# Mixer A probabilities of the sample tiles: from TensorE transposes to a round trip through DRAM and a 32x32 block transpose on VectorE

## The reference, cut to what matters

```
z = h @ w_in                       # q, k, v, gates of both mixers; h = modulated RMS norm of x
# mixer A, 8 heads, each with two 64-wide halves c of q and k; v is 128 wide
s = einsum('bqhcd,bshcd->bhcqs', q, k) / sqrt(64)
p = softmax(s, axis=-1)
p = p[:, :, 0] - lam[h] * p[:, :, 1]
o = einsum('bhqs,bshe->bqhe', p, v)      # sample: 512 + 256 keys; prompt: 128 keys
o = rms_norm(o, subln) * (1 - lam_init) * silu(gate)
y = rms_norm(x + gate_ada * (concat(o_A, o_B) @ w_out), g_final)
```

## Time and profile before

| | |
|---|---|
| median of 3 runs | 1253.91 us (1253.86 to 1254.21) |
| span of the profiled execution, first to last instruction | 1253.5 us |
| its own time outside the span | not shown; the median lies 0.4 us above the span |
| TensorE busy | 1222.7 us, 98% |
| VectorE, ScalarE, POOL busy | 800.0 (64%), 619.1 (49%), 258.3 us (21%) |
| chain of work that ended last | 92% TensorE |
| transposes of p on TensorE | 400 of 128x128, 192 of them for mixer A's sample tiles |

### The profile page before, as it was taken

The page is one execution under the profiler, slowest core; times in us unless marked ns, Lnnn a source line. Parts: engine busy times, 40 slices in busy tenths (PEclk is TensorE's granted clock), DMA queues, the critical chain, the costliest instruction groups (busy, mean ns, idle before and its releaser), DMA issues.

```text
span 1253.5 us, 16906 instructions
## 1 busy us (share of the span) xinstructions
PE 1222.7 (98%) x6251; PEld 991.3 (79%) x6251; DVE 800.0 (64%) x1242; ACT 619.1 (49%) x1296; POOL 258.3 (21%) x439
## 2 busy tenths in 40 slices
PE   5899999999999999999999999999999999999996
PEld 3455778888888888888888888888888888888885
DVE  4455488667586776755546374554647675789774
ACT  5522325645555465565556555656556765312223
POOL 1211033012031040222221221222223322211111
PEclk9999999999999999999999999999999999999998
DMA  9999242222221232322222121222224423756544
GB/s 348 371 377 349 84 110 76 62 71 74 76 96 44 67 106 53 100 60 83 71 61 86 51 91 51 82 59 83 59 72 133 139 83 98 254 187 228 184 135 177
DMA packets 130482, 156.45 MB, mean 125 GB/s; under 512 B 8304, under 2 KB 97040, under 8 KB 129632
## 3 DMA queue, kind: packets, MB, share of 16 engines
q1 hardware_dynamic: 116528, 109.60, 26.7%
q0 software_dynamic: 13424, 45.20, 11.4%
q10 hardware_dynamic: 448, 0.57, 0.1%
HBM read 144.18 MB, written 11.16 MB: 124 GB/s over the span
## 4 chain that ended last, share of the span: by engine, by line
PE 92%; SPq 3%; DVE 2%; DMA 1%; ACT 1%; POOL 1%; issue 0%; POOLq 0%; DVEq 0%; ACTq 0%
PE z_ps L704 24%; PE z_ps L706 23%; PE z_ps L705 23%; PE ring L795 5%; PE ring L884 4%; SPq L658 2%; PE ring L829 2%; PE ring L828 2%; PE ring L730 2%; PE ring L888 2%; DMA ada_raw<-in_w_ada_dram 1%; PE ring L706 1%; PE ring L705 1%; PE ring L891 1%; PE ring L704 1%
## 5 line engine op out<-in xcount | busy, mean ns | idle before, releaser
L704 PE MATMUL z_ps<-w_hi,xt_hi 128*128 128x512 f32 x1350 | 554.1, 410 | 2.6 <-issue 1.1
L706 PE MATMUL z_ps<-w_hi,xt_lo 128*128 128x512 f32 x1350 | 527.7, 391 | 0.0
L705 PE MATMUL z_ps<-w_lo,xt_hi 128*128 128x512 f32 x1350 | 527.2, 391 | 0.0
L1007 ACT ACTIVATE w_hi<-w_raw 128x512 fp32r<-128x512 f32 x270 | 169.3, 628 | 334.9 <-PE z_ps L706 309.2
L704 PEld LDWEIGHTS z_ps<-w_hi,xt_hi 128*128 128x128 f32 x1350 | 254.0, 188 | 68.1 <-issue 27.2
L1441 DVE TENSOR_TENSOR w_lo<-w_raw,w_hi 128x512 fp32r<-128x512 f32 x270 | 196.8, 732 | 162.6 <-ACT w_hi L1007 162.2
L706 PEld LDWEIGHTS z_ps<-w_hi,xt_lo 128*128 128x128 f32 x1350 | 253.4, 188 | 55.3
L705 PEld LDWEIGHTS z_ps<-w_lo,xt_hi 128*128 128x128 f32 x1350 | 254.8, 189 | 38.8
L1542 DVE TENSOR_REDUCE small<-s_sb 128x2 f32<-128x1536 f32 (+1 forms) x60 | 87.6, 1460 | 20.6 <-ACT s_sb L1007 20.6
L1153 ACT ACTIVATE s_sb<-s_sb,small 128x768 f32<-128x768 f32 (+1 forms) x120 | 98.0, 821 | 3.6 <-DVE small L1542 3.5
L1902 POOL TENSOR_TENSOR sg<-sg,zs 128x128 f32<-128x128 f32 (+1 forms) x60 | 38.6, 644 | 276.2 <-DVE sg L1511 275.6
(11 more groups left out here) (196 smaller groups left out, 1378.3 us busy)
## 6 DMA issues: line engine op xcount, KB each, us to landing
w_raw<-in_w_in_dram SPq DMA_DIRECT2D x188, 256.0 KB, 3.1
ada_raw<-in_w_ada_dram SPq DMA_DIRECT2D x64, 512.0 KB, 11.6
w_raw<-in_w_out_dram SPq DMA_DIRECT2D x64, 256.0 KB, 3.8
gate_raw<-in_w_ada_dram POOLq DMA_DIRECT2D x12, 1024.0 KB, 8.0
w_raw<-in_w_in_dram POOLq DMA_DIRECT2D x20, 256.0 KB, 6.3
o_spill<-row_st POOLq DMA_DIRECT2D x14, 320.0 KB, 3.4
row_st<-o_spill POOLq DMA_DIRECT2D x14, 320.0 KB, 3.3
x_sb<-in_x_sample_dram SPq DMA_DIRECT2D x4, 1024.0 KB, 9.6
```

What stands on the lines that cost most here:

```text
L704: pe.matmul(out, hi_l, hi_r, start=start, stop=False)
L705: pe.matmul(out, hi_l, lo_r, start=False, stop=False)
L706: return pe.matmul(out, lo_l, hi_r, start=False, stop=stop)
L1007: return act.activation(out, in_, ACT.Copy, **kw)
```

## The change

For the sample tiles of mixer A (t > 0, 32 tiles) the piece T has no TensorE work any more. ScalarE writes the scores in another order of columns (by quadrant i, key block k, 32 columns b). When the combine is done, SP stores the 128x768 tile to DRAM (`p_spill`), waits until it has landed, and loads it back in four DMAs, one for each group of 32 partitions, so that the 32x32 blocks stand in their places. One `transpose` on VectorE (`turn_blocks`) then turns every block and writes `pt_f`. It stands in the step where T stood, after `gated`. V(t) waits for it by `p_turned`. ScalarE's two copies from PSUM are gone; the third score copy becomes two. SP's program interleaves these transfers with its weight loads. In the last pass S(0) comes in step 3 instead of 4, S in 3, 4, 6, 8, 9 and V in 6, 8, 10, 12, 13. Tile 0 and mixer B stay as they were.

```diff
+LAST_STEPS = {
+    1: [("O", -1)], 2: [("QK", 0)], 3: [("S", 0)], 4: [("S", 1)], 5: [("T", 0)], 6: [("S", 2), ("V", 0)], 7: [("T", 1)],
+    8: [("S", 3), ("V", 1)], 9: [("T", 2), ("S", 4)], 10: [("V", 2)], 11: [("T", 3)], 12: [("V", 3), ("T", 4)], 13: [("V", 4)],
+    14: [("O", 0)], 15: [],
+}
+LAST_PLACES = {12: [2], 13: [4], 14: [2, 3]}
...
     if kind == "T":
-        return (2 if t else 1) * (2 if g == "G" and t else 1)
+        return 0 if by_blocks(a, t) else (2 if t else 1) * (2 if g == "G" and t else 1)
...
+            def move_blocks(a, t):
+
+                b, n = t % 2, p_count(a, t)
+                sp.wait_ge(p_ready, n_step(a, t) + 1)
+                sp.dma_start(p_spill[b], s_sb[:, b, 0, :]).then_inc(p_out[b], 16)
+                if n > 1:
+                    sp.wait_ge(p_turned, turns_before(a, t) - 1)
+                else:
+                    wait_full(sp, TURN[("V", D_IT - 1, TILES - 1)])
+                sp.wait_ge(p_out[b], 16 * n)
+                for i in range(QUAD):
+                    src = p_spill[b].rearrange("(j b) (i n) -> i b j n", j=QUAD, i=QUAD)[i]
+                    sp.dma_start(p_blocks[b][SUB * i:SUB * (i + 1), :, :], src).then_inc(p_in[b], 16)
...
+            for q in range(OPEN, len(ORDER)):
+                moves = [(a, t) for kind, a, t in steps_at(*ORDER[q - 1]) if kind == "S" and by_blocks(a, t)]
+                if moves:
+                    while j <= min(q // 2 + 3, len(ORDER) // 2 - 1):
+                        load_w(sp, j)
+                        j += 1
+                for a, t in moves:
+                    move_blocks(a, t)
...
                     wait_free(pe, m)
+                if by_blocks(a, t):
+                    pe.wait_ge(p_turned, turns_before(a, t) + 1)
...
+                if by_blocks(a, t):
+                    if t > 2:
+                        act.wait_ge(p_out[t % 2], 16 * p_count(a, t - 2))
...
+            def turn_blocks(a, t):
+
+                b = t % 2
+                dve.wait_ge(p_in[b], 16 * QUAD * p_count(a, t))
+                wait_full(dve, TURN[("V", a, t - 1)])
+                dve.transpose(pt_f[:, :].rearrange("p (k j b) -> p j k b", k=KB, j=QUAD),
+                              p_blocks[b][:, :, :].rearrange("p j (k b) -> p j k b", k=KB)).then_inc(p_turned, 1)
...
                     for kind, a, t in old:
                         if kind == "V":
                             gated(a, t)
+                for kind, a, t in late:
+                    if kind == "T" and by_blocks(a, t):
+                        turn_blocks(a, t)
```

More of the change, by code:

```diff
@@ L111, with by_blocks @@
 STEPS_D[2] = [("QK", 0)]
[L113 to L121, removed]
+LAST_STEPS = {
[4 more added lines that the diff above has]
+LAST_PLACES = {12: [2], 13: [4], 14: [2, 3]}
+QUAD, KB, SUB = 4, LAT + PAST, P // 4
+def by_blocks(a, t):
+    return t > 0 and group_kind(a) == "D"
 def group_kind(a):
@@ L303, in build @@
     gate_rows = nc.dram_tensor("gate_rows", (2, D_MODEL), F32).ap()
+    p_spill = nc.dram_tensor("p_spill", (2, P, NKEY), F32).ap()
     at = [(nc.sbuf_base + 31) // 32 * 32]
@@ L349, in build @@
     pt_f, _ = place("pt_f", [P, NKEY], F32, pt0)
+    p_blocks = [place(f"p_blocks{i}", [P, QUAD, KB * SUB], F32, pt0 + 4 * NKEY * (1 + i))[0] for i in range(2)]
     v_f, _ = place("v_f", [P, 7, DH], F32, pt0 - 4 * 7 * 2 * DH)
@@ L434, in build @@
         pt_hi_done = sem("pt_hi_done")
+        p_turned = sem("p_turned")
+        p_out, p_in = ([sem(f"{w}{b}") for b in range(2)] for w in ("p_out", "p_in"))
         o_part, o_sq, o_rstd, og_ready = sem("o_part"), sem("o_sq"), sem("o_rstd"), sem("og_ready")
@@ L537, in t_parts, with p_count, turns_before, quads @@
                 return [(n, c, 0, 1, P * c, c == heads(a) - 1) for c in hs]
+            if by_blocks(a, t):
+                return []
             return [(n + 2 * c + j // 4, c, j, m, 0, True) for c in hs for j, m in ((0, 4), (4, 2))]
+        def p_count(a, t):
+            return 2 * (a - D_IT) + (t - 1) // 2 + 1
+        def turns_before(a, t):
+            return (TILES - 1) * (a - D_IT) + t - 1
+        def quads(row):
+            return row.rearrange("p (i k b) -> p k i b", i=QUAD, b=SUB)
         PT_BEFORE = {}
@@ L673, in _ @@
                 load_ada(n)
-            for j in range(EARLY_PAIRS, ITS * KT // 2):
+            def move_blocks(a, t):
[10 more added lines that the diff above has]
+                    sp.dma_start(p_blocks[b][SUB * i:SUB * (i + 1), :, :], src).then_inc(p_in[b], 16)
+            j = EARLY_PAIRS
+            for q in range(OPEN, len(ORDER)):
[6 more added lines that the diff above has]
+                    move_blocks(a, t)
+            for j in range(j, ITS * KT // 2):
                 load_w(sp, j)
@@ L1127, in scores_out @@
                     act.wait_ge(zr_ready, a + 1)
+                if t == 0 and a > D_IT:
+                    act.wait_ge(p_out[0], 16 * p_count(a - 1, 4))
+                if t == 1 and a > D_IT:
+                    act.wait_ge(p_out[1], 16 * p_count(a - 1, 3))
+                if by_blocks(a, t):
+                    if t > 2:
+                        act.wait_ge(p_out[t % 2], 16 * p_count(a, t - 2))
+                    for c_ in range(2):
+                        wait_full(act, n + c_)
+                        copy(quads(s_sb[:, t % 2, c_, :])[:, 0:LAT],
+                             RB(n + c_)[:, :].rearrange("p (k i b) -> p k i b", k=LAT, i=QUAD),
+                             scale=DK_A ** -0.5).then_inc(free_sem(n + c_), 1)
+                    wait_full(act, n + 2)
+                    for c_ in range(2):
+                        ins = copy(quads(s_sb[:, t % 2, c_, :])[:, LAT:],
+                                   RB(n + 2)[:, PAST * P * c_:PAST * P * (c_ + 1)].rearrange("p (k i b) -> p k i b", k=PAST, i=QUAD),
+                                   scale=DK_A ** -0.5)
+                    ins.then_inc(free_sem(n + 2), 1)
+                    return
                 if group_kind(a) == "D":
```

## The result

| | before | after |
|---|---|---|
| median, same chip | 1253.94 us (5 runs, 1253.86 to 1254.21) | 1258.78 us (5 runs, 1257.04 to 1261.31) |
| ratio | | 1.0037, 95% interval 1.0025 to 1.005 |
| span of the profiled execution | 1253.5 us | 1257.0 us |
| TensorE busy | 1222.7 us | 1210.0 us |

I forecast 1246.8, faster. The changed kernel is slower by 4.8 us in the medians, 3.5 of them between the two traced executions. The rest is mostly a mistake of reading: other executions of the kernel before, taken beside the later experiments, have 1.6 us between device time and span (1254.16 and 1252.5, for one), and after has 1.8 (1258.78 and 1257.0). By that the traced execution of before took some 1255.1 us (an estimate from these numbers), about 1.2 over the median; I had taken it for the median itself, with 0.4 us outside the span.

The account below looks back on a forecast made before the run. TensorE, without a gap in a mixer A pass, was taken as the bound. Six ordinary passes gain 10.6 us, the seventh loses 2.1, the last 1.4: 7.1 off 1253.9 gives 1246.8, range 1237 to 1259.

Parts of the forecast that it names:

- TensorE's gain, 0.68 us a tile: Without a sample tile's six transposes TensorE saves 0.68 us, 2.72 a head, 21.8 for 32 tiles if nothing is late.
- The turn, d = 1.0: VectorE's block transpose of one 128x768 tile takes 1.0 us, the time of a two-input row of the same size.
- Rival 3: The turn on VectorE takes 1.6 us or more: 1.7 us slower at 1.6, 1262 us at 2.0; chance 0.10.
- V1 behind og, 0.96 an ordinary pass: In step 8 the turn for V1 waits for og of tile 0, so TensorE stalls 0.96 us in each ordinary pass.
- Rival 1: Nothing is late at V1, as POOL's root or og comes sooner: 17 us off, 1237 us; chance 0.12.
- V2 to V4 no stall, L = 6.9: Store plus four loads take 6.9 us (5.5 to 9.5), in time by 0.5 us, so later V pieces don't wait.
- Seventh pass, net -2.1; V1 3.84, V3 0.7, V4 0.2: With spilled rows also returning, stalls before V1, V3 and V4 exceed the 2.72 us gain: a net loss of 2.1.
- Last pass, S0 2.8: S0, moved to step 3, waits 2.8 us for the doubled q from VectorE's casts; the pass loses 1.4 net.
- V2's 0.4: Last pass, step 9: tile 4's maximum stands ahead of og(V1) and the turn, delaying V2 by 0.4 us (0 to 1.7).
- V3 and V4 have room: In the re-timed last pass V3 and V4 were taken to have slack, with no stall.
- rival 2: The store and load round trip is late at V4, 8 times: 0.8 us per 0.1 over 7.4, up to 1264; chance 0.15.
- one of my signs of being wrong: Listed signs: turn over 1.2 us, idle before V4, VectorE waiting at the turn for a DMA, or w_lo late for TensorE.

Follow-up runs that it names:

- the turn first: The changed kernel with VectorE's block turn of a tile placed ahead of `gated` in its step: median 1251.47 us, ratio 0.9975 to the kernel before.
- seven heads: Blocks in the six ordinary passes and the seventh, turn ahead of `gated`, last pass as in the kernel before: 1243.41 us, ratio 0.9908.
- S0 later: The changed kernel with S of tile 0 in the last mixer pass behind the last tile of step 3, not the first: 1253.74 us, ratio 0.9994.
- six heads: Blocks in the six ordinary passes only, turn ahead of `gated`, seventh and last passes and steps as in the kernel before: 1238.08 us, ratio 0.9868.

## Why the prediction was wrong

- **TensorE's gain, 0.68 us a tile:** right; 0.70 measured.
- **The turn, d = 1.0:** right; 0.97. Rival 3 falls.
- **V1 behind og, 0.96 an ordinary pass:** right in cause and price; 0.91, of which the rows show 0.66 as idle. Rival 1 falls. Six passes gave 11.3 us, where I had 10.6.
- **V2 to V4 no stall, L = 6.9:** right for the ordinary passes (L is 5.9).
- **Seventh pass, net -2.1; V1 3.84, V3 0.7, V4 0.2:** the idles were 3.62, 0.23 and 0.74, in all as forecast. The net was -5.6, for the fall behind V1 (1.7) and QK's 1.25 were missing. That the forecast idles came near was in part luck: the kernels with the turn first and with seven heads show that a second lateness hid behind V1. I had taken L from ordinary passes, while in this one rows of 320 KB are loaded too, and DMA engines are busy 0.59 of the time.
- **Last pass, S0 2.8:** right as an idle, 2.79. Its price was 4.3 with the fall (QK to V0, S0 later). V2's 0.4 did not come, and O's 0.65 was left out.
- **"V3 and V4 have room":** this step failed. I counted the time from combine to V and left out what else the DMA engines do then. x_add and gate_b slow the round trip of tile 3 to 13 us (store issued 1049.20, turn 1062.25). This is rival 2, at a place it did not name: the last pass, once, and not V4 eight times. It also is one of my signs of being wrong: VectorE waits at the turn for a DMA, 5.00 us for tile 3 and 4.10 for tile 4.
- **No term for the order of the PSUM banks:** QK's 1.25, read below.
- **No term for the clock:** the other failure. I priced idles by their length. Each of the three of about 3 us costs 1.6 to 1.7 us more.

The last two passes cost 15.0 us where I had 3.5. Of the 11.5 between, three falls are about 5, V3 is 3.64, QK 1.25 and O 0.65; the 1 left is of the size of what brackets leave out (some 0.25 at each V1).

QK waits for xt_lo in all ten traces with the seventh pass by blocks (0.98 to 1.27 us), and in none of the four without. VectorE is not later there: its row starts 4.4 us after O in both kinds (1002.19 and 1006.57 after, 991.40 and 995.81 with six heads). With six heads QK starts before that row:

```profile
995.42 0.60 PE L844 MATMUL ring<-ident,zs 128*128 128x128 f32 x4
...
995.81 0.89 DVE L1704 TENSOR_TENSOR xt_lo<-ring,xt_hi 128x512 fp32r<-128x512 f32 x2
```

The code tells why. The pieces take three PSUM banks in turn, beginning at bank 0 with each QK (`count_turns`). Without the two banks that T took for each sample tile, O of a head falls on banks 2 and 0 instead of 1 and 2, and QK of the next head begins with bank 0. The seventh head's O is read by VectorE itself (`rows_lo`, heads whose result is not spilled), and QK has to wait for that read. No run changed the order of the banks alone, so this cause is read from code and starts, and not tried.

## What to carry to other kernels

A store to DRAM with a load back can take several times as long beside other large transfers: size it in each stage by what is loaded there, above all where a large load of another engine's queue falls in it, and use it only where there is slack. Put what the bottleneck waits for ahead of what nobody waits for in the order of a helping engine: here one move gave 0.9 us a pass. When work goes away, see which buffers the rest now falls on. And an idle of some 3 us on TensorE costs more than its length, so a change that trades steady work for one long wait can lose although it removes more than it adds.

## What the runs showed of the hardware

- **The granted clock after an idle.** Over all traces: no low clock behind any TensorE idle of up to 1.7 us (V1 to V4, QK, O); behind those of 2.68 to 2.91 us sometimes, with the same 2.83 us before S0 once none and once 3.0 us lost; behind every one of 3.08 to 5.72 us, some 1.7 us lost, but 2.3 once. The Trainium skill's page "TensorE: Matmul & The Clock Gate", section "Part 1: The HAM clock gate", says that half clock is the state of an idle array and that activity lifts it; the traces agree in this, at 1.2 and 2.4 GHz.
- **The 32x32 block transpose** of 128x768 float32 on VectorE takes 0.97 us (0.92 at the shortest row shown). The Trainium skill's page "VectorE: DVE Perf Modes", section "Rules for kernel authors", advises TensorE for a 128x128 transpose where PSUM will do. With TensorE as the bound and a round trip that is hidden, the other way was better here, by 2.8 us a head.
- **The round trip:** in the changed kernel a 384 KB store takes 2.3 us and a 96 KB load 2.2 at the median; 3.4 and 3.5 in the seventh pass of the kernel with seven heads, up to 8.5 and over 8 beside x_add.
